# A second expert's first tile, computed amid the last routing of a mixture-of-experts stage

## What is computed

```python
def hier_moe(x, w_rg, w_re, w_gate, w_up, w_down):     # x: the normed rows, 2112 of them
    pg = softmax(xt @ w_rg)                            # 4 expert groups: the best one
    g_idx = argmax(pg);  g_w = pg[rows, g_idx]
    le = (xt @ w_re).reshape(nt, 4, 4)                 # 4 experts in each group: the best two
    pe = softmax(le[rows, g_idx])
    top_w, top_i = top_k(pe, 2)
    ...
    h = silu(einsum('td,edf->tef', xt, w_gate)) * einsum('td,edf->tef', xt, w_up)
    h = h * combine[..., None]                         # 0 for the 14 experts that a row did not pick
    return einsum('tef,efd->td', h, w_down)            # 16 experts: 1024 -> 256 -> 1024
```

## Time and profile before

| what | us |
|---|---|
| median of 3 runs | 838.98 |
| lowest, highest | 837.78, 839.27 |
| the profiled execution | 839.68 |
| its span, first to last instruction | 837.9 |

### The profile page before, as it was taken

The page is one execution under the profiler, slowest core; times in us unless marked ns, Lnnn a source line. Parts: engine busy times, 40 slices in busy tenths (PEclk is TensorE's granted clock), DMA queues, the critical chain, the costliest instruction groups (busy, mean ns, idle before and its releaser), DMA issues.

```text
span 837.9 us, 15253 instructions
## 1 busy us (share of the span) xinstructions
PE 788.5 (94%) x4234; PEld 620.9 (74%) x4234; DVE 596.1 (71%) x1129; ACT 412.5 (49%) x770; POOL 322.2 (38%) x416
## 2 busy tenths in 40 slices
PE   5999999999999999999858999999999999999983
PEld 4878876656778787787646888888888888878762
DVE  7997789996534364547855688678876788876863
ACT  6466753124335453442414566446664476665631
POOL 3900001002000002305243567766666666666532
PEclk9999999999999999999977999999999999999996
DMA  8465315888743242433356577675856768875822
GB/s 311 143 212 191 126 22 161 228 170 204 277 151 127 100 151 89 140 124 105 118 196 224 166 266 278 227 264 190 313 193 220 276 222 309 291 254 198 289 95 79
DMA packets 57401, 161.29 MB, mean 192 GB/s; under 512 B 21584, under 2 KB 26192, under 8 KB 50640
## 3 DMA queue, kind: packets, MB, share of 16 engines
q1 hardware_dynamic: 34032, 112.99, 41.6%
q0 software_dynamic: 22976, 47.05, 16.1%
q10 hardware_dynamic: 288, 0.03, 0.0%
HBM read 129.06 MB, written 62.40 MB: 228 GB/s over the span
## 4 chain that ended last, share of the span: by engine, by line
PE 43%; DVE 3%; issue 3%; DVEq 1%; ACT 1%; ACTq 1%; POOL 0%; POOLq 0%
PE pbig L1321 8%; PE pbig L1322 8%; PE pbig L1325 8%; PE pbig L1340 4%; PE pbig L1341 4%; PE pbig L1342 4%; PE pbig L1294 4%; PE pbig L1333 1%; DVE WL L1924 0%; DVE hh L1777 0%; ACT WH L912 0%; ACT xgH L922 0%; DVEq L2024 0%; PE pbig L1310 0%; ACTq L280 0%
## 5 line engine op out<-in xcount | busy, mean ns | idle before, releaser
L1321 PE MATMUL pbig<-WH,xgH 128*128 x312 | 128.6, 412 | 1.4 <-ACT xgH L922 1.4
L1322 PE MATMUL pbig<-WL,xgH 128*128 x312 | 124.5, 399 | 0.0
L543 POOL DMA_INDIRECT records<-rec,at_rec x34 | 34.8, 1024 | 196.0 <-DVEq L1917 186.9
L1241 PE MATMUL pbig<-w2H,ysH 128*128 128x512 f32 x256 | 105.2, 411 | 0.0
L1242 PE MATMUL pbig<-w2L,ysH 128*128 128x512 f32 x256 | 100.7, 393 | 0.0
L1243 PE MATMUL pbig<-w2H,ysL 128*128 128x512 f32 x256 | 100.4, 392 | 0.0
L607 POOL DMA_INDIRECT x_sums<-xg,recs x36 | 71.7, 1993 | 42.0 <-DVE xg L2021 36.5
L1924 DVE SCALAR_TENSOR_TENSOR WL<-WR,gf_p,WH 128x512 f32 (+1 forms) x128 | 86.1, 746 | 0.1
L912 ACT ACTIVATE WH<-WR,gf_p 128x512 f32 (+1 forms) x128 | 80.4, 711 | 1.6
L1325 PE MATMUL pbig<-WH,xgL 128*128 x312 | 79.1, 396 | 0.0
L2021 DVE SCALAR_TENSOR_TENSOR xg<-pbig,recs,xg 128x1024 f32<-128x1024 f32 x39 | 49.9, 1280 | 30.1 <-PE pbig L1342 30.1
(11 more groups left out here) (334 smaller groups left out, 1716.0 us busy)
## 6 DMA issues: line engine op xcount, KB each, us to landing
WR<-in_w_gu SPq DMA_DIRECT2D x32, 1024.0 KB, 6.9
WR<-in_w_dn SPq DMA_DIRECT2D x16, 1024.0 KB
xT<-in_x_cols SPq DMA_DIRECT2D x16, 512.0 KB, 3.6
low<-in_x_rows SPq DMA_DIRECT2D x16, 512.0 KB, 4.3
U<-in_x_rows SPq DMA_DIRECT2D x16, 512.0 KB, 5.3
x_mid<-x SPq DMA_DIRECT2D x16, 512.0 KB, 2.7
x_sums<-x SPq DMA_DIRECT2D x16, 512.0 KB, 4.3
w<-in_w_out SPq DMA_DIRECT2D x1, 4096.0 KB, 13.7
```

The lines of the kernel that those rows point to most:

```text
L1241: pe.matmul(pbig[:, n, :], ysH[b][:, k, :], w2H[n][:, k, :], start=(k == 0), stop=False)
L1321: pe.matmul(pbig[:, 6, :], xgH[b][:, k, :], WH[:, ds(off + k * 2 * DE, 2 * DE)], start=(k == 0), stop=False)
L1322: pe.matmul(pbig[:, 6, :], xgH[b][:, k, :], WL[:, ds(low_ + k * 2 * DE, 2 * DE)], start=False, stop=False)
```

## The change

The first tile of expert 1 is treated as expert 0's is. `extra` has two values, so that the first tile of each of the two is full after tile 11; the two first tiles' records are read early from the table, and the rows of both are gathered amid the projection. The slots' order becomes: slot 0 is expert 0's first tile, slot 1 expert 1's first tile, slots 2 and 3 expert 0's other tiles, slot 4 expert 1's other tile, slots 5 and 6 expert 2's, and all later slots as before. Slots 0 and 1 need no control words, so the words are computed for slots from 2 on (`slotc` starts at -2, the totals of experts 0 and 1 count without their first tile). `C_NEXT` is never set in an expert-0 slot; in expert 1 it is set in the first of its other tiles.

Expert 1's weights are cut by fixed addresses, without control words, and slot 1's up products stand around the control words and slot 0's down products. `turn_bank` gives slot 1's turned rows other banks.

```diff
-SLOTS = (2 * NT + (NE + 1) * (P - 1)) // P
+SLOTS = 2 * NT // P + NE + 1
...
+        def turn_bank(s, n):
+            return ((2, 3), (3, 7), (4, 5))[min(s, 2)][n]
...
-                if t == 1:
+                if t == 2:
                     pool.wait_ge(S["tab_first"], 32)
                     pool.wait_ge(S["ctl_done"], 1)
...
                     gather(0)
+
+                    pool.wait_ge(S["a_done"], 4 * TF - 1)
+                    gather(1)
...
-            for t in range(1, AHEAD):
+            for t in range(2, AHEAD):
                 gather(t)
...
             e_silu(0, 0)
+
+            for b in range(2):
+                act.wait_ge(S[f"x2_st{b}"], 32 * (TF // 2) + 64 * (1 - b))
+            act.wait_ge(S["lt_done"], TT)
+            act.wait_ge(S["wts0"], 32)
+            cut_hi(0, 0)
             e_ht_hi(0, 0)
-
+            e_x(1, 1)
+            act.wait_ge(S["idx_done"], len(BATCHES))
+            act.wait_ge(S["rl_done"], TT)
+            act.wait_ge(S["wts1"], 32)
+            cut_hi(0, 1)
+            act.wait_ge(S["tab_in"], 16 * 2 * (TT - FIRST_TOK))
             act.wait_ge(S["ctl_done"], 1)
+            act.wait_ge(S["wts2"], 32)
+            cut_hi(0, 2)
+            e_silu(1, 1)
+            e_ht_hi(1, 1)
+            e_x(2, 0)
...
-            now = e_words(0)
-            e_x(1, 1)
-            e_cut(0, *now, (0, 1))
-            for s in range(1, FULL - 1):
+            now = None
+            for s in range(2, FULL - 1):
                 now = e_act(s, s % RING, now)
...
+            def second_turn(n):
+
+                pe.wait_ge(S["gat1"], 16)
+                pe.wait_ge(S["xgt_evac"], 2)
+                pe.wait_ge(S["xgt_lo"], 2)
+                if n == 1:
+                    pe.wait_ge(S["pos_read"], len(BATCHES))
+                for k in range(4):
+                    mm = pe.transpose(pbig[:, turn_bank(1, n), k * P:(k + 1) * P], xg[1][:, (4 * n + k) * P:(4 * n + k + 1) * P], ident[:, :])
+                mm.then_inc(S["xgt_done"], 1)
+
+            def up_second_hi(lo, hi):
+
+                if lo == 0:
+                    pe.wait_ge(S["rl_evac"], TT)
+                    pe.wait_ge(S["xgt_evac"], 4)
+                for k in range(lo, hi):
+                    pe.wait_ge(S["hi_split"], PIECES + k + 1)
+                    pe.matmul(pbig[:, 6, :], xgH[1][:, k, :], WH[:, k * 2 * DE:(k + 1) * 2 * DE], start=(k == 0), stop=False)
+
+            def up_second_lo():
+
+                pe.wait_ge(S["xgt_lo"], 4)
+                for k in range(KD):
+                    pe.matmul(pbig[:, 6, :], xgL[1][:, k, :], WH[:, k * 2 * DE:(k + 1) * 2 * DE], start=False, stop=False)
+                for k in range(KD):
+                    pe.wait_ge(S["lo_split"], PIECES + k + 1)
+                    mm = pe.matmul(pbig[:, 6, :], xgH[1][:, k, :], WL[:, EW + k * 2 * DE:EW + (k + 1) * 2 * DE], start=False, stop=(k == KD - 1))
+                mm.then_inc(S["gu_done"], 1)
...
-            e_turn(1, 1)
-            now = None
-            for s in range(1, FULL - 1):
+            e_turn(2, 2)
+            now = (0, 1, EW)
+            for s in range(2, FULL - 1):
                 now = e_step(s, s % RING, now)
...
-            dch(ts(ne, pbig[:, 4, 0:NE], float(P - 1), None, ALU.add))
+            dch(tt(ne, pbig[:, 4, 0:NE], more, ALU.add))
...
+            dch.go(ts(two_, e15, 1.0, None, ALU.is_le))
+            dch.go(ts(one_, e15, 1.0, None, ALU.is_ge))
             dch(ts(f_, h_, 0.0, None, ALU.is_equal))
             dch.go(ts(g_, e15, float(NE - 1), None, ALU.is_lt))
+            dch.go(tt(f_, f_, one_, ALU.mult))
+            dch(tt(col, col, two_, ALU.add))
...
```

More of the change, by code:

```diff
@@ L44 @@
 FULL = 2 * NT // P
-GAP = 960
+GAP = 944
 WORDS = 5
@@ L220, in hybrid_kernel @@
         slotc = sb("slotc", [P, 1])
-        te = sb("te", [P, 6, NE])
+        te = sb("te", [P, 8, NE])
         tei = sb("tei", [P, 2, NE], I32)
-        wv = sb("wv", [P, 12])
+        wv = sb("wv", [P, 16])
         wvi = sb("wvi", [P, 2], I32)
         words_f = sb("words_f", [P, WORDS])
-        extra = sb("extra", [P, 1])
+        extra = sb("extra", [P, 2])
         wr_sb = sb("wr_sb", [P, KD, 32])
@@ L445, in _ @@
                     sp.wait_ge(S["tab_early"], 16 * 2 * FIRST_TOK)
-                    sp.dma_start(tab[:, 0:1, :], table[:, 0:1, :]).then_inc(S["tab_first"], 16)
+                    firsts = [t[:, 0:2 * TT, :].rearrange("p (e c) w -> p e c w", e=2)[:, :, 0, :] for t in (tab, table)]
+                    sp.dma_start(*firsts).then_inc(S["tab_first"], 16)
             weights(1)
@@ L563, in gather @@
                 r, q = t % RING, t % 4
-                if t:
+                if t > 1:
                     fetch(t)
@@ L921, in e_x @@
                     act.wait_ge(S["xgt_done"], 2 * s + n + 1)
-                    act.activation(xgH[b][:, 4 * n:4 * n + 4, :], pbig[:, (4 if s else 2) + n, :].rearrange("p (a m) -> p a m", a=4), ACT.Copy).then_inc(S["xgt_evac"], 1)
+                    act.activation(xgH[b][:, 4 * n:4 * n + 4, :], pbig[:, turn_bank(s, n), :].rearrange("p (a m) -> p a m", a=4), ACT.Copy).then_inc(S["xgt_evac"], 1)
             def e_silu(s, b):
@@ L927, in e_silu @@
                     act.wait_ge(S["h_done"], s)
-                else:
-                    act.wait_ge(S["rec_set"], 1)
+                if early(s):
+                    act.wait_ge(S["rec_set"], s + 1)
                 act.activation(sl[:, :], pbig[:, 6 if s else 0, 0:DE], ACT.Silu, scale=recs[:, s, ROOT:ROOT + 1]).then_inc(S["sl_done"], 1)
@@ L1414, in _ @@
             pe.nop().then_inc(S["dn_done"], 1)
+            second_turn(0)
             e_hturn(0, 0)
+            second_turn(1)
+            up_second_hi(0, KD // 2)
             pe.wait_ge(S["words_set"], 1)
@@ L1421, in _ @@
             e_down(0, 0, EW, 0, 0)
+            up_second_hi(KD // 2, KD)
+            up_second_lo()
+            e_hturn(1, 1)
             pe.wait_ge(S["ctl_done"], 1)
@@ L1433, in e_step @@
                 now, b = words(s), r % 2
-                if before:
+                if s > 2:
                     e_hturn(s - 1, 1 - b)
@@ L1437, in e_step @@
                 e_turn(s + 1, (r + 1) % RING)
-                if before:
-                    e_down(s - 1, 1 - b, *before)
+                e_down(s - 1, 1 - b, *before)
                 return now
@@ L1830, in _ @@
             dch(dve.memset(te[:, 0, :], 1.0))
+            dch(dve.memset(te[:, 5, :], float(P - 1)))
+            dch(dve.memset(te[:, 5, 0:2], -1.0))
+            dch(dve.memset(te[:, 6, :], 1.0))
+            dch(dve.memset(te[:, 6, 0:1], 0.0))
             def route_a(n):
@@ L1868, in route_a @@
                     if t == FIRST_TOK:
-                        dch(tt(EP[0:1, t, 0:1], EP[0:1, t, 0:1], extra[0:1, :], ALU.add))
+                        dch(tt(EP[0:1, t, 0:2], EP[0:1, t, 0:2], extra[0:1, :], ALU.add))
                 dve.nop().then_inc(S["d_ready"], 1)
@@ L1905, in route_b @@
                 if n == 1:
-                    dch(ts(extra[0:1, :], pbig[0:1, 7, 256:257], -1.0, float(P), ALU.mult, ALU.add))
+                    dch(ts(extra[0:1, :], pbig[0:1, 7, 256:258], -1.0, float(P), ALU.mult, ALU.add))
                     dch(ts(extra[0:1, :], extra[0:1, :], 0.0, None, ALU.max))
@@ L1962, in _ @@
             ne, nti, ntf, cum, mask, begs = tei[:, 0, :], tei[:, 1, :], te[:, 1, :], te[:, 2, :], te[:, 3, :], te[:, 4, :]
-            e_, beg, e15, h_, u_, col, at_, nx, f_, g_ = (wv[:, k:k + 1] for k in range(10))
+            more, least = te[:, 5, :], te[:, 6, :]
+            e_, beg, e15, h_, u_, col, at_, nx, f_, g_, two_, one_ = (wv[:, k:k + 1] for k in range(12))
             ei, par_ = wvi[:, 0:1], wvi[:, 1:2]
             dve.wait_ge(S["tot_done"], 1)
-            dch(ts(ne, pbig[:, 4, 0:NE], float(P - 1), None, ALU.add))
+            dch(tt(ne, pbig[:, 4, 0:NE], more, ALU.add))
             dch(ts(nti, ne, 7, None, ALU.logical_shift_right))
-            dch(ts(ntf, nti, 1.0, None, ALU.max))
+            dch(tt(ntf, nti, least, ALU.max))
             dch(dve.tensor_tensor_scan(cum, te[:, 0, :], ntf, 0.0, ALU.mult, ALU.add))
@@ L2088, in e_rest @@
                     dve.nop()
-            now = e_words(0)
             e_x_lo(1, 1)
-            e_cut(0, *now, (0, 1))
-            for s in range(1, FULL - 1):
+            for c in range(UP_CUTS):
+                cut_lo(0, EW, 1, c)
+            e_h(1, 1)
+            e_sum(0, 0)
+            e_ht(1, 1)
+            e_x_lo(2, 0)
+            cut_lo(0, EW, 1, UP_CUTS)
+            now = None
+            for s in range(2, FULL - 1):
                 now = e_step(s, s % RING, now)
```

18 lines of the change are left out of this document (9 added, 9 removed).

## The result

| what | before | after |
|---|---|---|
| median of 4 runs, us | 838.95 | 844.04 |
| lowest, highest | 837.78, 839.27 | 841.66, 845.03 |
| profiled execution's span | 837.9 | 839.5 |

The ratio is 1.006, 95% interval 1.004 to 1.008: the change costs 5.1 us (3.4 to 6.7). The forecast was 841.7 with a range of 839.1 to 845.6, and slower at 0.68. A second measurement of the same kernel, on another occasion (e4), gave 843.32 and 1.0049 (1.003 to 1.0067).

What follows compares the result with a forecast made beforehand. TensorE, busy 94%, was taken as the bound, so its idle or half-clocked time had to go. Losses of 8.3, 2.6 and 1.65 less a gain of 9.8 made 2.75 us longer: 841.7 us, range 839.1 to 845.6.

Steps and rivals of the forecast that it cites:

- Late cut, first stall: Before slot 5's up products: TensorE waits for all eight of VectorE's low pieces of expert 2's weights, 8.3 us.
- Half clock behind it: Slot 5's up products: the clock falls during the first stall and they run slow after it, 2.6 us lost.
- the 2.4 us of idle that left the clock whole: Premise for the clock's fall: 2.4 us of idle inside window 410 to 414 were not followed by half clock.
- Second stall: Slot 5's step holds two cuts, expert 2's down part and expert 3's up parts, delaying slot 6's `hh`: 1.65 us.
- The sum of the loss: First stall 8.3, half clock 2.6 and second stall 1.65, total 12.55 us.
- Gain of the fill: At 430 to 465 us: slot 1's up products fill TensorE's hole, slot 2's hidden rows turned 9.8 us earlier.
- the landing of slot 2's gather: In the fill: gathered at 437.9, landing 4.2 to 6.0 us later, at 442.1 to 443.9, so just hidden.
- the 2.1 from the turn to the up products: In the fill: from the start of slot 2's turn to its first up product, 2.1 us at full clock.
- no half clock behind it: Slot 2's up products in the fill: a full-clock step of 9.34 us to the turn of its hidden rows.
- rival (b): In the fill: expert 2's load delays slot 2's gather and the clock falls; gain only 5.4, 846.1 us; chance 0.13.
- Rival (a): At fill and first stall: the clock is kind, gain 11.0 and little loss at the stall; 838.4 us; chance 0.21.
- Rival (c): Expert 2's cut is not late, so both stalls and the second clock loss fall away; 829.2 us; chance 0.06.

Runs made afterwards that it cites:

- e1: The changed kernel with expert 2's up weights cut in slot 3's step instead of slot 4's, its down part in slot 4's, by slot number: 831.09 us, ratio 0.9915.
- e2: The kernel before, with only expert 2's cut moved from expert 1's first slot to its second: 851.35 us, ratio 1.0144.
- e3: The changed kernel with 32 unread products added on TensorE in the wait before slot 5's up products: 841.96 us, ratio 1.0032.
- e11: e1 with expert 2's down part cut one slot later, in slot 5's step, ahead of expert 3's up parts: 832.71 us, ratio 0.993.
- e9: The changed kernel with the load of expert 2's weights held until slot 2's rows have landed, late cut kept: 843.89 us, ratio 1.0051.
- e10: The changed kernel with expert 2's cut placed earlier by control words for any counts, and its load held until slot 2's rows have landed: 828.04 us, ratio 0.9869.
- e12: e9 with 11 unread products added: four behind slot 1's up products, seven behind the turn of slot 2's rows: 840.96 us, ratio 1.002.
- e6: e1 with the load of expert 2's weights held until slot 2's gather has landed: 826.98 us, ratio 0.987.

## Why the prediction was right, and where it was off

- **Late cut, first stall: right.** Forecast 8.3 from the end of VectorE's pieces against the start of the up products; from h4 to the up products it is 8.45 in place of 0.13, so 8.32, with the wait named as foreseen. e1 takes it away, e2 brings it into the kernel before.
- **Half clock behind it: right.** Forecast 2.6; the up products and what follows took 12.11 up to h5 in place of 9.34, so 2.77, and e3 shows 2.8. Once TensorE went on, the half clock lasted some 6.1 us (484.94 to 490, and half of the next two). The estimate by the rule of the Trainium skill (TensorE: Matmul & The Clock Gate, Terms) is then 3.05, 0.3 over the measured loss. Counted from the clock's fall at 480.8, idle time and all, the throttled time would be 10.2 us and the estimate 5.1, far from what this trace shows. The measurement decides. One of the prediction's premises was misread: the 2.4 us of idle that left the clock whole did not lie inside the window 410 to 414, whose row has 2.0; the wait was 2.36 and ended at 414.33. It changes no term.
- **Second stall: right, with a tail left out.** Forecast 1.65 (its own terms make 1.61). The step with the wait took 1.53 more than 9.43, in the changed kernel as in e11, and the step after it another 0.3, where the forecast had VectorE catch up at no cost. Together that is 1.85 (e11: 1.86), within the bounds of 1.4 to 2.
- **The sum of the loss** was forecast as 12.55. It is 12.7 by the trace (the three terms make 12.9, against the changed kernel's own steps of 9.43 in place of 9.47), 12.2 and 12.5 by the runs.
- **Gain of the fill: mis-sized.** Forecast 9.8 with bounds 9.3 and 11.0; the trace shows 7.1, e4 6.95, outside the bounds. That is nearly the whole error of the sum: 12.7 - 7.1 in place of 12.55 - 9.8. Three steps of it failed, each by a little. First, the landing of slot 2's gather was "just hidden" with 4.2 to 6.0. It went out 13.95 behind R in place of 13.49 (437.9 less 424.41) and took 6.14 beside the load, so T came 20.1 behind R in place of the forecast 19.5 (443.9 less 424.41). Slot 1's hidden rows (19.33) would have let it start at 19.6: e9, e10 and e12, which have no wait there, show 0.28 between the two turns. Second, the 2.1 from the turn to the up products was read where the control words had been read in the shadow of another wait; it was 2.78. Third, the forecast had no half clock behind it, since TensorE had been busy; the up products began at half and the step took 10.79 in place of 9.34. 0.6, 0.65 and 1.45 make the 2.7. Nothing cancelled in the sum: 844.04 lies above the forecast's own band (840.2 to 843.5) and inside the range because that took in the shades of rival (b).
- **Rival (b)** had the right mechanism, the load beside the gather and then the clock. Its switch was put at a landing at about 444, and the landing was at 444.05. What it did not foresee is that the clock could fall without the late gather (e9). It should have had a greater chance than 0.13: its shades, 843 to 846, hold the measured 844.04.
- **Rival (a)**, a kind clock, did not come true at the stall in any trace with the 8.07 us wait. Its loss behind that wait was between 1.8 and 2.8 (the step from h4 to h5 took 19.5 to 20.6). At the fill, of the kernels without added products, only e6 and e10 had it whole. **Rival (c)** is what e1 made by hand: forecast 829.2, measured 831.09, less by the same mis-sized fill.

## What to carry to other kernels

When a piece of work is pulled forward into a hole, look at what else takes its place by that order: here a word computed from the slot's position set the cut of the next weights, and the cost (12.5 us) began some 20 us behind the end of the gain (7 to 8). With the cut moved forward too, the same fill is 0.8 to 1.0% faster than before. A gain in front of a wait of 1 to 2 us may vanish in the clock behind it, so judge it over several executions and not by one trace, and try to fill the wait as well.
